# Attention of the second block in pairs of heads, on row and column parts of the TensorE array

## What is computed

```python
h = rmsnorm_2(x, norm_g)
z = h @ w_in_2                       # 31 column blocks of 128 in the kernel
# indexer: 8 heads of 32, keys shared by the heads
dots = einsum('bqhd,bsd->bqhs', iq, ik)
score = einsum('bqh,bqhs->bqs', iw, relu(dots))
sel = top 128 of the admissible scores per query
# "sparse": 6 heads of 64, softmax over the selected keys
# "decay": 6 heads of 64, causal, logits + F[t] - F[s], F = cumsum(log f)
s = q @ k.T / 8 ; p = softmax(s) ; o = p @ v
x = x + concat(pooled, sparse * silu(g), decay * silu(g)) @ w_out_2
out = rmsnorm_2(x, final_g)
```

## Time and profile before

| what | value |
|---|---|
| median of three runs | 1493.7 us |
| profiled execution: time / span | 1496.4 us / 1494.6 us |
| TensorE busy | 1448.2 us (97%) |
| VectorE, ScalarE, GpSimd busy | 822.1 (55%), 565.2 (38%), 184.7 us (12%) |
| granted TensorE clock, mean | 0.991 |
| chain that ended last, by engine | PE 88%, DVE 8%, ACT 2% |
| unit matmuls in the chain (L574) | 66% |

### The profile page before, as it was taken

How to read it: one execution, slowest core, us unless ns; L and a number is a source line. 1 busy time by engine, 2 the same in 40 slices (tenths; PEclk the granted TensorE clock), 3 DMA queues, 4 the chain that set the end, 5 groups by cost and what they waited for, 6 DMA issues and landing times.

```text
span 1494.6 us, 20211 instructions
## 1 busy us (share of the span) xinstructions
PE 1448.2 (97%) x7191; PEld 1183.2 (79%) x7191; DVE 822.1 (55%) x1399; ACT 565.2 (38%) x879; POOL 184.7 (12%) x257
## 2 busy tenths in 40 slices
PE   6899999999999999999989999999998899999998
PEld 4788888888888888888867888888886667777776
DVE  4556464646465555434436665346554688954532
ACT  4424242423434242222324443234444545545432
POOL 2101010101001010000032000000014153232300
PEclk8999999999999999999999999999999999999999
DMA  4222222222222221333322332333224222222211
GB/s 145 57 57 71 57 70 56 56 56 70 56 56 70 56 56 56 85 93 104 99 85 67 93 94 84 99 113 98 82 80 119 59 55 59 57 58 70 57 57 71
DMA packets 208501, 111.46 MB, mean 75 GB/s; under 512 B 6826, under 2 KB 206793, under 8 KB 208457
## 3 DMA queue, kind: packets, MB, share of 16 engines
q1 hardware_dynamic: 208073, 110.86, 26.2%
q0 software_dynamic: 384, 0.03, 0.0%
HBM read 108.75 MB, written 2.10 MB: 74 GB/s over the span
## 4 chain that ended last, share of the span: by engine, by line
PE 88%; DVE 8%; ACT 2%; issue 1%; POOL 0%; DMA 0%; DVEq 0%; ACTq 0%; POOLq 0%
PE gb L574 66%; PE gd L700 3%; PE gd L697 2%; PE gd L688 2%; PE gd L915 2%; PE gb L966 1%; PE gd L966 1%; PE gd L894 1%; DVE selb L1708 1%; DVE small L1707 1%; DVE act_a L1348 1%; PE gd L905 1%; DVE selb L1697 1%; PE gd L586 1%; PE gd L660 1%
## 5 line engine op out<-in xcount | busy, mean ns | idle before, releaser
L574 PE MATMUL gb<-act_a,whi 128*128 128x512 f32 x2800 | 974.9, 406 | 9.1 <-ACT act_a L989 4.5
L574 PEld LDWEIGHTS gb<-act_a,whi 128*128 128x128 f32 x2800 | 527.0, 189 | 127.1 <-DVE act_a L1348 10.8
L574 PE MATMUL gb<-act_a,wlo 128*128 128x512 f32 x1488 | 581.4, 391 | 0.0
L574 PEld LDWEIGHTS gb<-act_a,wlo 128*128 128x128 f32 x1488 | 281.7, 189 | 55.2 <-issue 4.1
L981 ACT ACTIVATE whi<-raw 128x1024 fp32r<-128x1024 f32 x212 | 223.0, 1052 | 226.7 <-PE gb L574 196.9
L1319 DVE TENSOR_TENSOR wlo<-raw,whi 128x1024 fp32r<-128x1024 f32 x190 | 233.4, 1229 | 129.3 <-ACT whi L981 128.9
L574 PE MATMUL gb<-act_b,whi 128*128 128x512 f32 x304 | 109.2, 389 | 0.0
L1954 POOL TENSOR_TENSOR wlo<-raw,whi 128x1024 fp32r<-128x1024 f32 x22 | 52.7, 2397 | 145.8 <-ACT whi L981 145.8
L574 PEld LDWEIGHTS gb<-act_b,whi 128*128 128x128 f32 x304 | 57.1, 188 | 11.9
L1862 POOL TENSOR_TENSOR rr<-ss,eps_head 128x4 f32<-128x4 f32 x8 | 1.6, 201 | 493.0 <-DVE ss L1476 493.0
L688 PEld LDWEIGHTS gd<-Ti,LT 128*128 128x128 f32 x384 | 50.2, 191 | 3.9
(11 more groups left out here) (401 smaller groups left out, 1603.9 us busy)
## 6 DMA issues: line engine op xcount, KB each, us to landing
raw<-in_w_in_dram SPq DMA_DIRECT2D x103, 512.0 KB, 3.6
raw<-in_w_up_dram SPq DMA_DIRECT2D x44, 512.0 KB, 3.7
raw<-in_w_down_dram SPq DMA_DIRECT2D x16, 384.0 KB, 3.2
raw<-in_w_down_dram SPq DMA_DIRECT2D x16, 320.0 KB, 3.0
raw<-in_w_a_out_dram SPq DMA_DIRECT2D x8, 512.0 KB, 3.5
raw<-in_w_b_out_dram SPq DMA_DIRECT2D x8, 512.0 KB, 3.5
raw<-in_w_o_dram SPq DMA_DIRECT2D x8, 512.0 KB, 3.5
raw<-in_w_out_dram SPq DMA_DIRECT2D x8, 512.0 KB, 3.4
```

The source lines that it names most:

```text
L574: ins = pe.matmul(gb[:, b, :], l, r, start=(first and m == 0), stop=(last and m == len(todo) - 1))
```

## The change

Plan: scores stand four at a time, in every second quarter (14, 16, ... 24); their matmul uses 32 rows, `ik4` holding the index keys at the four row offsets in one tile (the zero padding and its four memsets on GpSimd go); four PSUM banks instead of two. Heads go in pairs: both heads' `s` of a chunk stand in one quarter, chunks are four quarters apart; `weigh` and `t` of the odd head stand one quarter after those of the even one. The sparse heads' s uses 64 rows each; the memsets at L1762 go. One `pv` per pair, 19 quarters after its start, alternates between the heads' matmuls. The odd head's pT lies in four separate tiles (`pTs`), one copy for each block. The order numbers follow (`pair_step`). The rest of the diff carries the same renumbering to the other engines.

```diff
-        put((14 + n // 2) // 4, (14 + n // 2) % 4, ("score", n, c, h))
+        put((14 + n // 4 * 2) // 4, (14 + n // 4 * 2) % 4, ("score", n, c, h))
...
-    for t in range(2 * GROUPS):
-        start = 4 * 6 + 1 + 8 * t
+    for g in range(GROUPS):
+        start = 4 * 6 + 1 + 16 * g
         for c in range(TC):
-            todo.setdefault(start + 2 * c + 2, []).append((5, ("weigh", c, t)))
-            todo.setdefault(start + 2 * c + 4, []).append((0, ("t", c, t)))
-            todo.setdefault(start + 2 * c, []).append((3, ("s", c, t)))
-        todo.setdefault(start + 11, []).append((1, ("pv", 0, t)))
-        if t % 2 == 0:
-
-            todo.setdefault(start + (3 if t < 2 * GROUPS - 2 else 9), []).append((2, ("turn_v", t // 2)))
+            for t in (2 * g, 2 * g + 1):
+                todo.setdefault(start + 4 * c + 2 + t % 2, []).append((5, ("weigh", c, t)))
+                todo.setdefault(start + 4 * c + 4 + t % 2, []).append((0, ("t", c, t)))
+                todo.setdefault(start + 4 * c, []).append((3, ("s", c, t)))
+        todo.setdefault(start + 19, []).append((1, ("pv", g)))
+
+        todo.setdefault(start + (3 if g < GROUPS - 1 else 9), []).append((2, ("turn_v", g)))
...
+def pair_step(c, t):
+
+    return 2 * TC * (t // 2) + 2 * c + t % 2
...
+        pTs = ([pT[:, j, :] for j in range(TC)], [flat(Ui), flat(Ti), ob[:].rearrange("p c j -> p (c j)"), pT_odd[:]])
...
-                    if n >= 2:
-                        pe.wait_ge(relu_ready, n - 1)
-                    pe.matmul(gd[:, n % 2, 0:(c + 1) * P], iq[h // 4][:, c * P:c * P + P], ikz[h % 4][:, 0:(c + 1) * P],
+                    if n >= 4:
+                        pe.wait_ge(relu_ready, n - 3)
+                    elif n >= 2:
+                        pe.wait_ge(f_rows if n == 2 else f_tok, 1)
+                    r = slice(32 * (h % 4), 32 * (h % 4) + 32)
+                    pe.matmul(gd[:, n % 4, 0:(c + 1) * P], iq[h // 4][r, c * P:c * P + P], ik4[r, 0:(c + 1) * P],
                               start=True, stop=True).then_inc(score_done, 1)
...
-                        if t == 0:
-                            pe.wait_ge(relu_ready, (TC - 1) * IDX_HEADS)
-                    n = TC * t + c
+                        if t < 2:
+                            pe.wait_ge(relu_ready, (TC - 1) * IDX_HEADS - 3 + t)
+                    n = pair_step(c, t)
...
-                    pe.matmul(gd[:, c % 2, 0:(c + 1) * P], q[:, c * P:c * P + P], ring(g, 2 + i)[:, 0:(c + 1) * P],
+                    r = slice(0, P) if g < 3 else slice(64 * i, 64 * i + 64)
+                    pe.matmul(gd[:, i, 0:(c + 1) * P], q[r, c * P:c * P + P], ring(g, 2 + i)[r, 0:(c + 1) * P],
                               start=True, stop=True).then_inc(s_done, 1)
...
+                    if n == 0:
+                        pe.wait_ge(relu_ready, (TC - 1) * IDX_HEADS - 1)
...
                     for j in range(TC):
-                        ins = pe.matmul(gd[64 * i:64 * i + 64, 3, j * P:T], vt[g % 2][:, j, 64 * i:64 * i + 64],
-                                        pT[:, j, j * P:T], start=(j == 0), stop=(j == TC - 1))
-                    ins.then_inc(pv_done, 1)
+                        for i in range(2):
+                            ins = pe.matmul(gd[64 * i:64 * i + 64, 3, j * P:T], vt[g % 2][:, j, 64 * i:64 * i + 64],
+                                            pTs[i][j][:, j * P:T], start=(j == 0), stop=(j == TC - 1))
+                            if j == TC - 1:
+                                ins.then_inc(pv_done, 1)
...
+                    if t % 2 == 0:
+                        sc.activation(pT[:, 0:c + 1, c * P:c * P + P],
+                                      gd[:, 2, 0:(c + 1) * P].rearrange("p (j q) -> p j q", q=P), ACT.Copy).then_inc(pT_ready, 1)
+                    else:
+                        for j in range(c + 1):
+                            ins = sc.activation(pTs[1][j][:, c * P:c * P + P], gd[:, 2, j * P:j * P + P], ACT.Copy)
+                        ins.then_inc(pT_ready, 1)
...
-                        if g in (3, 4):
-
-                            for row in (64 - 64 * i, 96 - 64 * i):
-                                dve.memset(ring(g, 2 + i)[row:row + 1, :], 0.0)
...
-            for i in range(4):
-                ins = pool.memset(ikz[i], 0.0)
-            link(ins)
+            pool.wait_ge(xr_ready, 2)
```

More of the change, by code:

```diff
@@ L74 @@
 W_ORDER = (5, 6, 7, 2, 3, 4, 0, 1)
+TO_2K = 40
 MASKED = -3.0e38
@@ L1248, in beside @@
                     sc.wait_ge(score_done, n + 1)
-                    sc.activation(relu[n % 2][:, 0:(c + 1) * P], gd[:, n % 2, 0:(c + 1) * P], ACT.Relu).then_inc(relu_ready, 1)
+                    sc.activation(relu[n % 2][:, 0:(c + 1) * P], gd[:, n % 4, 0:(c + 1) * P], ACT.Relu).then_inc(relu_ready, 1)
                 elif what == "turn_v":
@@ L1259, in beside @@
                     _, c, t = e
[L1260 removed]
+                    n = pair_step(c, t)
                     sc.wait_ge(max_ready, n + 1)
[L1262 to L1263 removed]
+                    if n >= 4:
+                        sc.wait_ge(p_turned, n - 3)
                     elif n == 2:
@@ L1266, in beside @@
                     w = (c + 1) * P
-                    sc.activation(prob[c][:, 0:w], gd[:, c % 2, 0:w], ACT.Exp, bias=small[:, 8 + c:9 + c], scale=-1.0,
-                                  accum_out=small[:, 12 + c:13 + c]).then_inc(exp_ready, 1)
+                    k = n % 4
+                    sc.activation(prob[k][:, 0:w], gd[:, t % 2, 0:w], ACT.Exp, bias=small[:, 8 + k:9 + k], scale=-1.0,
+                                  accum_out=small[:, 12 + k:13 + k]).then_inc(exp_ready, 1)
                 elif what == "t":
                     _, c, t = e
-                    n = TC * t + c
+                    n = pair_step(c, t)
                     sc.wait_ge(p_turned, n + 1)
[L1273 to L1276, removed]
+                    if t >= 2 and c == 0:
+                        sc.wait_ge(pv_done, t // 2 * 2)
+                    if t % 2 == 0:
[5 more added lines that the diff above has]
+                        ins.then_inc(pT_ready, 1)
                 elif what == "pv":
-                    t = e[2]
-                    if t % 2:
-                        mixed(t // 2, (5, 6, 7, 2, 3, 4)[t // 2])
+                    mixed(e[1], (5, 6, 7, 2, 3, 4)[e[1]])
             for u in range(len(Z_UNITS)):
@@ L1721, in beside @@
                     dve.wait_ge(s_done, n + 1)
-                    dve.tensor_tensor_reduce(gd[:, c % 2, 0:w], gd[:, c % 2, 0:w], bias, -1.0, -MASKED, ALU.add,
-                                             ALU.min, small[:, 8 + c:9 + c]).then_inc(max_ready, 1)
+                    dve.tensor_tensor_reduce(gd[:, t % 2, 0:w], gd[:, t % 2, 0:w], bias, -1.0, -MASKED, ALU.add,
+                                             ALU.min, small[:, 8 + k:9 + k]).then_inc(max_ready, 1)
                 elif what == "weigh":
                     _, c, t = e
-                    n = TC * t + c
+                    n = pair_step(c, t)
+                    k = n % 4
                     dve.wait_ge(exp_ready, n + 1)
-                    link(dve.reciprocal(small[:, 24 + c:25 + c], small[:, 12 + c:13 + c]))
-                    p = prob[c][:, 0:(c + 1) * P]
-                    dve.tensor_scalar(p, p, small[:, 24 + c:25 + c], None, ALU.mult).then_inc(p_ready, 1)
+                    link(dve.reciprocal(small[:, 24 + k:25 + k], small[:, 12 + k:13 + k]))
+                    p = prob[k][:, 0:(c + 1) * P]
+                    dve.tensor_scalar(p, p, small[:, 24 + k:25 + k], None, ALU.mult).then_inc(p_ready, 1)
                 elif what == "window":
@@ L1734, in beside @@
                 elif what == "pv":
[L1735 to L1743 removed]
+                    g = e[1]
+                    dve.wait_ge(pv_done, 2 * g + 2)
+                    dve.wait_ge(z_read, G_READ[g])
+                    if g:
+                        dve.wait_ge(m_lo, g)
+                    dve.tensor_tensor(ot[:], gd[:, 3, :], sg[g % 2][:], ALU.mult).then_inc(ot_ready, 1)
+                    low(g, (5, 6, 7, 2, 3, 4)[g])
             def low(i, k):
```

29 lines of the change are left out of this document (10 added, 19 removed).

## The result

The changed kernel takes 1498.5 us (median of 14 runs, 1496.36 to 1503.77), the kernel before 1495.73 in its 14 runs beside them (1493.47 to 1497.28). The ratio is 1.0022 [1.0013, 1.0031]: slower by 0.2%, where 0.8% faster was forecast, and outside the range. The profiled execution took 1498.6 us with a span of 1496.8 (before: 1496.4 and 1494.6).

A forecast was written before the change was run, and what follows sets the result against it. VectorE was taken to bound the kernel until the search rounds end, TensorE behind. Gains 5.3 + 7.1 + 0.7 less 1.0 and 0.6 made 11.5 us off the median 1493.7: 1482 us, range 1476 to 1497.

The forecast's parts named there:

- Part 2: Stretch up to the rounds' end, met at quarter 69: VectorE's work nearly unchanged, gain 2.3 + R = 5.3 us.
- R = 3: Scores, before the rounds: VectorE idle time recovered by earlier scores, 3 us, between 0 and 4.5.
- Part 3: p times v in column halves: 2.61 us a pair against 2.50 a head, gain 7.1 us behind quarter 69.
- Part 4: s of the sparse heads on row halves: net 0.3 us worse a pair, 1.0 us lost for three pairs.
- rival D: Tiles free of order: s halves entirely, R is 4.5, gain 16.2 us, 1477.5 us; chance 0.14.
- (c): ScalarE's copies of the odd head in up to four pieces: taken as 0; without cover 0.5 a pair, 3 us.
- (b): Last p times v no longer waits for the copy of pT, as its transposes come earlier: 0.7 us gained.
- (d): Eight memsets of 485 ns leave VectorE in front of the k copies; TensorE doesn't wait for them: 0.
- (e): Four memsets leave GpSimd before the second block, where it waits for others anyway: 0.
- A: Rival: no overlap of halves, a pair of p times v costs 4.65 us; 1497.2 us, slower; chance 0.16.
- C: Rival: each change of tile drains the array, 0.35 us each, 14 us more than A; 1511 us; chance 0.06.
- B: Rival: weight loads of halves not covered, 4.8 us a pair of p times v; 1494 us; chance 0.08.

The follow-up runs named there:

- experiment 2: Kernel before, with GpSimd's subtraction for the low part of the weights cut to 8 of 1024 columns: 1495.48 us, 1.0003 to the kernel before.
- Experiment 8: Kernel before with only the scores changed, four at a time on quarters of the array: 1497.49 us, 1.001 to the kernel before.
- the runs at 1480.7 and 1481.0: Changed kernel with GpSimd's subtraction cut to 8 columns, 1480.68 us; changed kernel with subtraction in four pieces and xT work in halves, 1480.97 us.
- experiment 10: Changed kernel with GpSimd's subtraction in four pieces, plus the last chunk's placement written twice to fill a TensorE wait: 1484.22 us, 0.9925 to the kernel before.
- experiment 11: Changed kernel with GpSimd's subtraction in four pieces, plus its two xT instructions in halves: 1480.97 us, 0.9901 to the kernel before.

## Why the prediction was wrong

**Two regimes, and VectorE as the bound of the first: right for the changed kernel.** TensorE's wait of 0.5 us for zs was the telling one, and it grew to 14.2. For the kernel before it was too strong: experiment 2 shows both engines about equally late there.

**The step that failed is Part 2's sentence "VectorE's work up to there is nearly the same before and after".** The work is the same; the time isn't. For the scaling in front of quarter 69 I took 0.35 us, from a quiet row of 0.29, and never asked where scalings and closing steps fall against GpSimd. They wait for its subtraction, in after for 14.4 us and in before for 3.2: a term of 11.2 us that the sum doesn't have. The stages put the price on it: up to the end of the rounds cutting the subtraction is worth 15.6 us to after and 1.2 to before. I had 5.3 us gained in front of quarter 69 and 8.1 were lost, 13.4 us. What is missing of the rest is 1.2 us behind quarter 69 and 1.6 in the tail, less the 2.4 in front of the scores, so 13.8 in all, and the spans say 2.2 + 11.5 = 13.7. I had a row that should have stopped me: in the earlier trace rows a 512-column scaling takes 0.68 us, where an undisturbed one of its form takes 0.49.

The Trainium skill, "SBUF — State Buffer", section "Who interferes with whom", has the rule: VectorE and GpSimd share a pair of ports that one instruction holds to its end; tensor_scalar can take the pair, its form that writes an accumulator can't, and a VectorE instruction with two inputs in SBUF contends with one of GpSimd that reads SBUF. The traces agree on each count: the ends coincide to 0.1 to 0.3 us, the accumulator form takes 747 ns beside a running subtraction, and the two-input sums lengthen beside the xT work. The ports themselves no trace shows. Weighed before the result, it would have said that a collision costs up to 2.4 us each and sent me to compare the two timelines.

**R = 3: there, but hidden by the collisions.** It was to be VectorE's idle time recovered by earlier scores. With the subtraction cut in both kernels the pairs end the rounds 4.0 us earlier (123.6 against 119.6), so some 4 us come, near the upper bound of 4.5. Experiment 8 has the scores alone and gains nothing, so it takes the pairs too; how the two share it wasn't tested. Behind the rounds the same two kernels differ by 9.6 us, where 2.3 + 6.2 = 8.5 were forecast. Together that is 13.6 us for 11.5, from one profile each, and it fits the runs at 1480.7 and 1481.0, which lie 1 us below my 1482.

**Part 3, p times v: mechanism right, slightly too dear.** 2.61 us forecast, 2.40 measured, even below my bound of 2.5. I let the passes start in order, each second pass covering the other head's first; they start together. A slip in Part 2: four heads in two pairs instead of five single ones is 12.5 - 5.2 = 7.3 us less in front of quarter 69, not 10. Nothing hung on it.

**Part 4, s of the sparse heads: wrong in sign.** From the start of the transposes to the end of the next unit matmul it is 2.50 us with 128 rows and 1.98 with halves at 512 columns, 1.97 and 1.66 at 384, 1.40 and 1.37 at 256, and 1.34 and 1.46 at 128, where halves lose: 0.74 us a pair gained, where 0.3 was to be lost. That is rival D's price (0.75 a pair). The gain of 5.0 us behind quarter 69 is still below 6.2. New there are 1.6 us of lower clock (experiment 10), 1.4 of a wait for the copies of the odd head's pT (L1292), which I had costed at 0 under (c), and 0.8 at L915, for which the profile names no releaser.

**Part 5.** (b) right: no wait for pT stands before the last p times v. (c) wrong by up to 1.4 us, see above. (d) and (e): nothing contradicts the 0.

**The rivals.** A and C fall by the starts that coincide, B by the 2.40 us a pair, where it has 4.8. A was meant as the way to a slower kernel and gave 1497.2, near the 1498.5 measured, for a reason that isn't there. B rests on the Trainium skill, "TensorE: Matmul & The Clock Gate", Part 3 (a load overlaps only where row groups differ); here column halves with the same rows load and run beside each other (at 1433.09 both passes start together), and the measurement decides. D was right on TensorE and had no term for VectorE either: none of my cases had one. Slower came true at a chance of 0.14.

## What to carry to other kernels

Before giving time back to the busiest engine, ask who is next and who can hold that one up: lay the timeline of VectorE's SBUF-to-SBUF instructions beside GpSimd's, since a schedule moved by a quarter changes which of them meet. Where the mean of a form didn't follow its size (1623 ns for 256 columns, 422 for 384), it was a collision here, not work. The cheap cure is to cut GpSimd's long instructions into pieces: the subtraction in four did nothing for the kernel before and was worth 14.4 us to the changed one, the xT work in halves another 3.1.

## What was not expected of the hardware

- Column halves with the same rows run side by side with starts at most 10 ns apart, fp32's second pass included: 2.40 us for two heads. Two row halves do four passes of 512 columns in 1.13 us, four row quarters do eight passes of 256 columns in 0.72 us.
- A scaling of 128x128, 0.29 us by itself, takes 2.43 beside GpSimd's subtraction. MAX8 and MATCH_REPLACE8 show no trace of it: at 512 columns 689 and 675 ns after, 690 and 676 before.
- The granted clock fell to its lower level after some waits of TensorE of 1.4 to 3.2 us, and after other waits of about 2 us it didn't (experiment 11, the kernel before); in experiment 11 a wait of 3.02 us had none behind it. The same group of 32 placements behind a wait of 2.1 us took 5.47 us in after and 3.84 in the kernel before.
